# Splitting one subtraction between the vector engine and GpSimd in a two-block transformer kernel

## The reference, cut to what matters

```python
def swiglu(x, w_gate, w_up, w_down):
    return (jax.nn.silu(x @ w_gate) * (x @ w_up)) @ w_down

def moe_swiglu(h, w_router, b_router, w_gate, w_up, w_down):
    ...
    logits = (t @ w_router).astype(jnp.float32) + b_router.astype(jnp.float32)
    top_v, top_i = lax.top_k(logits, TOP_K)
    top_w = jax.nn.softmax(top_v, axis=-1)
    ...
    for e in range(N_EXPERTS):
        out = out + gates[:, e:e + 1].astype(t.dtype) * swiglu(t, w_gate[e], w_up[e], w_down[e])
    return out.reshape(B, S, D)
```

## Time and profile before

| | |
|---|---|
| median of the runs (2) | 2517.18 us (2514.78 to 2519.57) |
| profiled execution, own time | 2516.98 us |
| its span, first to last instruction | 2515.2 us |
| TensorE busy | 2473.6 us, 98% |
| vector engine busy | 1863.8 us, 74% |
| of it the subtraction L1053 | 1258.2 us, 550 times |
| scalar engine busy | 1519.3 us, 60% |
| GpSimd busy | 0.2 us |
| transfers | 585.25 MB, 233 GB/s over the span |

### The profile page before, as it was taken

One profiled execution on the slowest core, in us unless ns is written; L12 is line 12 of the kernel. 1 busy time (PEld: TensorE's weight loads), 2 busy tenths in 40 slices (PEclk: granted clock), 3 DMA queues, 4 the chain that ended last, 5 costly groups with the idle time before them and its releaser, 6 DMA issues.

```text
span 2515.2 us, 38463 instructions
## 1 busy us (share of the span) xinstructions
PE 2473.6 (98%) x16646; PEld 2227.0 (89%) x16646; DVE 1863.8 (74%) x1635; ACT 1519.3 (60%) x1558; POOL 0.2 (0%) x4
## 2 busy tenths in 40 slices
PE   9999999999999999999999999999999999999998
PEld 8899999887888888888888888898999999899998
DVE  6765556867888888888888888756875565767655
ACT  6563436566777777777777777656654365575433
POOL 0000000000000000000000000000000000000000
PEclk9999999999999999999999999999999999999999
DMA  6335554324999999999999999533445544343552
GB/s 248 135 118 185 184 185 143 136 91 181 367 356 363 356 363 353 359 359 363 355 361 359 362 350 367 192 135 111 158 157 179 193 168 143 118 168 134 185 185 84
DMA packets 83313, 585.25 MB, mean 233 GB/s; under 512 B 9244, under 2 KB 11132, under 8 KB 12612
## 3 DMA queue, kind: packets, MB, share of 16 engines
q1 hardware_dynamic: 83140, 582.73, 62.1%
HBM read 581.64 MB, written 1.05 MB: 232 GB/s over the span
## 4 chain that ended last, share of the span: by engine, by line
PE 91%; DVE 5%; ACT 3%; issue 1%; DMA 0%; DVEq 0%; ACTq 0%
PE PS L1784 89%; DVE wlo L1053 2%; ACT whi L548 1%; PE PS L2305 1%; PE PS L1988 1%; DVE stat L1185 0%; DVE hT L1099 0%; ACT pb L661 0%; DVE lf L1239 0%; DVE pb L1210 0%; ACT pt L676 0%; DVE xT L1358 0%; DVE yT L1244 0%; DVE hlo L1069 0%; DMA raw<-in_ws 0%
## 5 line engine op out<-in xcount | busy, mean ns | idle before, releaser
L1053 DVE TENSOR_TENSOR wlo<-raw,whi 128x2048 fp32r<-128x2048 f32 x550 | 1258.2, 2291 | 380.4 <-ACT whi L548 371.0
L548 ACT ACTIVATE whi<-raw 128x2048 fp32r<-128x2048 f32 x550 | 1051.8, 1913 | 315.2 <-PE PS L1784 304.0
L1784 PE MATMUL PS<-hhi,whi 128*128 128x256 f32 x1984 | 573.1, 289 | 6.4 <-DVE wlo L1053 1.6
L1784 PE MATMUL PS<-hlo,whi 128*128 128x256 f32 x1984 | 561.7, 283 | 0.0
L1784 PE MATMUL PS<-hhi,wlo 128*128 128x256 f32 x1984 | 561.7, 283 | 0.0
L1784 PEld LDWEIGHTS PS<-hhi,whi 128*128 128x128 f32 x1984 | 380.4, 192 | 16.9 <-issue 12.2
L1784 PEld LDWEIGHTS PS<-hlo,whi 128*128 128x128 f32 x1984 | 380.4, 192 | 0.9 <-issue 0.4
L1784 PEld LDWEIGHTS PS<-hhi,wlo 128*128 128x128 f32 x1984 | 380.3, 192 | 0.0
L1784 PE MATMUL PS<-whi,xghi 128*128 128x512 f32 x896 | 360.0, 402 | 1.2 <-DVE wlo L1053 1.1
L1784 PE MATMUL PS<-whi,xglo 128*128 128x512 f32 x896 | 355.2, 396 | 0.0
L1784 PE MATMUL PS<-wlo,xghi 128*128 128x512 f32 x896 | 355.1, 396 | 0.0
(11 more groups left out here) (364 smaller groups left out, 3542.7 us busy)
## 6 DMA issues: line engine op xcount, KB each, us to landing
raw<-in_wm SPq DMA_DIRECT2D x336, 1024.0 KB, 5.3
raw<-in_ws SPq DMA_DIRECT2D x214, 1024.0 KB, 4.8
xT<-in_xT SPq DMA_DIRECT2D x4, 256.0 KB, 6.9
bsum<-in_bsum SPq DMA_DIRECT2D x1, 1024.0 KB
out_T<-hT SPq DMA_DIRECT2D x4, 256.0 KB, 2.5
lmask<-in_lmask SPq DMA_DIRECT2D x1, 512.0 KB
onehot_in<-in_onehot SPq DMA_DIRECT2D x1, 288.0 KB
lbw<-in_lbw SPq DMA_DIRECT2D x1, 256.0 KB
```

Of the source, the lines that this page charges most:

```text
L548: act.activation(whi[s % SPLIT][:], raw[s % RAW][:], ACT.Copy).then_inc(hi_ready, 1)
L1053: dve.tensor_tensor(wlo[s % SPLIT][:], raw[s % RAW][:], whi[s % SPLIT][:].bitcast(F32), ALU.subtract).then_inc(lo_ready, 1)
L1784: return pe.matmul(out, a, b, start=start, stop=stop, skip_group_check=True)
```

## The change

The subtraction `wlo = raw - whi` of each unit is cut by columns. The vector engine keeps columns 0 to 1535 and counts up `lo_ready` as before. GpSimd gets a program of its own: for each of the 550 units it waits for `hi_ready`, subtracts columns 1536 to 2047, and counts up a new semaphore `lo_rest_ready`. TensorE at each `take`, and SP before each load from the fifth on, now wait for both semaphores.

```diff
+REST = 512
...
+        lo_rest_ready = sem("lo_rest_ready")
...
                 if s >= RAW:
                     sp.wait_ge(lo_ready, s - RAW + 1)
+                    sp.wait_ge(lo_rest_ready, s - RAW + 1)
...
             def split_lo(s):
                 dve.wait_ge(hi_ready, s + 1)
-                dve.tensor_tensor(wlo[s % SPLIT][:], raw[s % RAW][:], whi[s % SPLIT][:].bitcast(F32),
+                most = slice(0, UNIT - REST)
+                dve.tensor_tensor(wlo[s % SPLIT][:, most], raw[s % RAW][:, most], whi[s % SPLIT][:, most].bitcast(F32),
                                   ALU.subtract).then_inc(lo_ready, 1)
...
+        def gpsimd_program(pool):
+            rest = slice(UNIT - REST, UNIT)
+            for s in range(U_ALL):
+                pool.wait_ge(hi_ready, s + 1)
+                pool.tensor_tensor(wlo[s % SPLIT][:, rest], raw[s % RAW][:, rest], whi[s % SPLIT][:, rest].bitcast(F32),
+                                   ALU.subtract).then_inc(lo_rest_ready, 1)
...
             def take():
                 s = stream.next() - 1
                 pe.wait_ge(lo_ready, s + 1)
+                pe.wait_ge(lo_rest_ready, s + 1)
                 return whi[s % SPLIT], wlo[s % SPLIT]
...
             block.vector(vector_program)
+            block.gpsimd(gpsimd_program)
             block.tensor(tensor_program)
```

## The result

The changed kernel takes 2539.14 us (2537.04 to 2541.25, 2 runs) against 2517.18: 1.0091 times the time before, 95% interval 1.0069 to 1.0113. It is slower by 22 us, within 2%, and 2 us from the 2537 predicted.

A forecast was written before the change was run, and what follows sets the result against it. TensorE, busy 2473.6 of 2515.2 us, was taken to bound the kernel. 2517 us plus 13 in the experts and 7 in the mixers gave 2537 us, +0.8%, with a range of 2497 to 2612.

The forecast's parts named there:

- The bound and the ceiling: Whole kernel: TensorE busy 2473.6 of 2515.2 us, so at most 41.6 us (1.7%) can be won.
- In turn: Each unit's subtraction: the engines exclude each other at SBUF, pair 2.937 us; likeliest case, chance 0.37, 2537 us.
- GpSimd's price: GpSimd's subtraction of 512 columns: taken as 1.15 us, between bounds of 0.69 and 2.29.
- the slower rival: Experts: pair too long for the beat; GpSimd at 1.26 us gives 3.147 us a unit, 2602 us, +3.4%; chance 0.32.
- Experts: Expert stretch: pair of 2.937 against 2.884 us a unit, 0.053 over in 240 units, 13 us lost; nothing in 96 others.
- Mixers: Mixers: later pairs +7, shorter subtractions -4, other vector instructions meeting GpSimd +4; together +7 us, ends -10 and +23.
- the 42% that come late: Mixers: 0.42 of 19 subtractions on the chain find GpSimd done and are 0.534 us shorter, -4 us.
- The holds: Mixers: +7 us from pairs ending 0.65 us later; other vector instructions meeting GpSimd 11 us at most, a third taken, +4.
- a sign of being wrong that the prediction named: Vector engine: other instructions growing longer by more than the 11 us put on them would prove the prediction wrong altogether.
- At nothing: Dense feed-forwards (5.9 us a unit, twice the pair), second waits, and `mact` and `malo`, which read PSUM: each costed at nothing.
- The second waits: TensorE and SP waiting for a second semaphore: costed at nothing; 0.03 us for 550 units would be 16 us.
- Side by side: Each unit's subtraction: both engines run at the same time; 2497 to 2507 us, no measurable change; chance 0.30.

The follow-up runs named there:

- write_only: Changed kernel with all its waits, but GpSimd fills a spare buffer with zeros instead of subtracting: 2510.48 us, 0.9976 times the kernel before.
- other_buffers: Changed kernel, but GpSimd subtracts 512 columns of a buffer no other engine touches into a spare one: 2524.19 us, 1.0035 times the kernel before.
- the three sizes run here: GpSimd's part of 256, 512 (the change) or 768 columns: 2521.33, 2539.14 and 2614.58 us; GpSimd alone takes 0.72, 1.27 and 1.81 us.
- experts_only: Changed kernel with the division made only for the 336 units of the experts, the other 214 subtracted whole by the vector engine: 2525.91 us, 1.0034.
- short: Kernel before, but from the fourth unit on nobody subtracts the last 512 columns and GpSimd has no program: 2510.75 us, 0.9979.
- rest_only_late: Changed kernel, division only for the 214 units outside the experts, GpSimd waiting for the vector engine's part instead of the rounding: 2533.24 us, 1.0075.
- 768 columns: Changed kernel with GpSimd taking 768 columns in place of 512, the vector engine 1280: 2614.58 us, 1.0388 times the kernel before.
- other_rounded: Changed kernel, but GpSimd subtracts a buffer no other engine touches into a spare fp32r buffer: 2525.96 us in one run.

## Why the prediction was right, point by point

**The bound and the ceiling: right, the ceiling too high.** TensorE sets the time; the gain alone is 6 us, not 10. The chain's 43 us of the subtraction were worth less than the quarter that I put on them. The vector engine's part itself is right: 1.757 us predicted, 1.759 in the median.

**In turn: right, and it was the open question.** I chose it on thin ground: equal rates with one and with two inputs in SBUF suggested that the vector engine has two ways in, and said nothing of GpSimd sharing one. What settled it are the durations of both engines here, then `write_only` (no reads, no turns) and `other_buffers` (other data, turns all the same). The rule of the Trainium skill ("SBUF — State Buffer", section "Who interferes with whom") says just this, the exception for a GpSimd instruction that only writes included, and the runs agree: 0.53 us beside a subtraction for the fill, 2.83 for the subtraction.

**GpSimd's price: nearly right.** I took 1.15 us between 0.69 and 2.29; it is 1.27 alone and 1.07 as a turn behind the vector engine. The pair is 1.76 + 1.07 with some 0.04 for the start, 2.87 us, against 2.937 predicted and a beat of 2.884. So it fits by a hair. That is partly luck: alone GpSimd is as slow as the slower rival had it (1.26), and 1.15 came near only because the fixed 0.18 us seem to pass in the wait, which no row before could show. The Trainium skill's "GPSIMD Engine Reference" (section "Performance versus the Vector engine") gives 4497 ns for 2048 columns; the line through the three sizes run here gives 0.18 + 2048 x 2.12 ns, 4.5 us, an estimate, and agrees.

**Experts: 13 predicted, 9 measured** (`experts_only`). The ordinary groups give 0.09 us each, 4 us in 40, where I had 0.3 each. The pair is under the beat, so this is no lack of throughput but the latency at the tightest place: in the group from 1015.68 the rounding of the third unit ends at 1018.12, GpSimd starts at 1018.19 and, at 2.8 us a unit, ends at about 1021.0, and TensorE starts that unit at 1021.17, about 0.1 us late. The other half stands in the first longer group of an expert, with its stop, which I had at nothing: I reckoned with that group's mean beat of 3.04, and the stop comes after its second unit. The chain has 7 of them (the last expert's result is carried back behind the stretch): at 0.57 us they are the other 4 us.

**Mixers: 7 predicted, about 13 to 17 measured: the step that was mis-sized, and a term that the sum did not have.** The gain is smaller. All 19 executions on the chain coming shorter were to give 10 us, and `short` gave 6, so the 42% that come late give some 2.5 (an estimate) in place of 4. The holds are larger. In the changed kernel the vector engine is busy 1733.2 us, in `short` 1586.0, so it was held 147 us, 93 of them on its subtraction (1061.4 against 968.0) and 54 on others. These are sums of busy time over the whole program, most of them off the chain; still, other vector instructions growing by more than 11 us was a sign of being wrong that the prediction named, and it is there. I had read the names of instructions only as far as the chain showed them; the products `sil<-sil,rstd` and `hT<-qkb,cosB` with two inputs were further down in the list. And I had counted instructions that read one buffer as free: `pb<-pb,stat` is one, apart from a column of factors, and its longest took 1.03 us where it was 0.36 before.

The missing term is TensorE's clock. By the measure used for `rest_only_late` it took 10.6 us of the changed kernel's profiled execution against 3.6 of the one before: 7 of the 24 us between their spans (2539.5 and 2515.2). With 8 in the experts, some 10 are left for the mixers at full clock, an estimate, near the 7 that I had. So the total came out 2 us off by luck: experts 4 too high, mixers 6 to 10 too low, a good part of it through a cause that I did not think of.

**At nothing: right.** The dense feed-forward's long piece of the chain is 236.81 us after and 236.82 before, though each of its units is in turn as well. (A unit there has 48 matmuls, not the 24 that I wrote: 1972 matmuls in 237 us for 41 or 42 units, 0.12 us each. The 5.9 us a unit stand; with 24 it would have been 2.9, and no cover.) The second waits are free (`write_only`). `mact` and `malo` read PSUM and were not held: 0.735 and 0.681 us after, 0.742 and 0.684 before.

**The slower rival** was as close as its threshold said: with 768 columns the pair misses the beat and the kernel is 3.9% slower. **Side by side** is refuted by the durations of both engines.

## What to carry to other kernels

Giving the quieter engine a quarter of the work took 131 us off the busy time of the vector engine and made the kernel slower: ask first which engine sets the end, then whether the two engines can read at the same time. Where they take turns, compare the sum of both parts, not the longer one, with the beat of the stretch; here 2.87 against 2.88 us cost 9 us, and 3.11 cost 63 of 98. Such a turn is not listed as a wait: it shows as a longer duration of the instruction that was held (0.69 us grown to 1.78). A bound on the gain (the work taken away and given to nobody) is a cheap experiment, and here it would have been reason enough not to divide: 0.2%.

## What the runs showed of the hardware

**TensorE's clock fell to its lower level behind a pause, and not every time.** In the attention of the second model TensorE waits for a vector engine instruction (`pb<-pb,nlam,pb`) before a block of 80 matmuls, and where that instruction is held the wait is longer. For each place, first the matmuls behind the wait, from the timeline (in brackets the time that TensorE was idle before them, in us), then the block, from the chain. The kernel before, `other_rounded`, the changed kernel (the same place in layers 0 and 1), and 768 columns:

```profile
1710.54 1.10 PE L1988 MATMUL PS<-ident,pb 128*128 128x128 f32 x8 [1.34 <-DVE pb L1189]
...
1711.64 9.09 PE PS L1784 x80
```

```profile
1714.08 1.09 PE L2003 MATMUL PS<-ident,pb 128*128 128x128 f32 x8 [1.40 <-DVE pb L1194]
...
1715.17 12.19 PE PS L1798 x80
```

```profile
1723.16 1.09 PE L2000 MATMUL PS<-ident,pb 128*128 128x128 f32 x8 [1.63 <-DVE pb L1193]
...
1724.26 13.72 PE PS L1795 x80
...
2191.97 1.10 PE L2000 MATMUL PS<-ident,pb 128*128 128x128 f32 x8 [1.63 <-DVE pb L1193]
...
2193.07 9.09 PE PS L1795 x80
```

```profile
1786.22 1.38 PE L2000 MATMUL PS<-ident,pb 128*128 128x128 f32 x8 [2.17 <-DVE pb L1193]
...
1787.60 13.47 PE PS L1795 x80
```

TensorE was idle for 1.34, 1.40, 1.63, 1.63 and 2.17 us; the blocks took 9.09, 12.19, 13.72, 9.09 and 13.47. The same 1.63 us had a fall behind them in one layer and none in the other, and 1.40 had one too: the length of the pause does not decide it alone, and what does is not shown. The stretches of the changed kernel (start:end, length, busy time by engine, then the granted clock):

```profile
1724.00:1738.00 14.00, 14.00 (x85) 11.94 (x84) 9.49 (x18) 7.38 (x21) 1.27 (x1) 0.63 0.20 76
...
2193.00:2203.00 10.00, 10.00 (x89) 8.88 (x88) 8.80 (x16) 7.48 (x22) 1.29 (x1) 1.00 0.28 107
```

The mean granted clock of 0.63 is a time at 1.2 GHz (0.50 from 1725 to 1730) and a rest at 2.4. One such spell costs 4.6 us, a fifth of the change's whole loss in the execution profiled. The two runs of the changed kernel are 4.2 us apart, and their mean granted clocks are 0.995 and 0.997: 0.002 of 2540 us is 5 us, one spell.

**GpSimd's subtraction of 512 columns took 1.04 us where both inputs were one buffer, 1.27 where they were two.** The one buffer also lay elsewhere and held the same number throughout, so the cause is open.
